# Prompt attention by position classes modulo 4, with scores in two halves of the TensorE array

## The reference

```
h = RMSNorm(x);  [u, Bg, Cg, q/k/v per head group, g_a, g_b] = h @ w_in
A = W_conv_out( Bg * dwconv3_causal( Cg * u ) )
B = W_attn_out( merge_g softmax-attn_g(q_g, k_g, v_g) )
x = x + W_o( sigmoid(g_a) * A + sigmoid(g_b) * B )
[up, gate] = RMSNorm(x) @ w_ffn_in;  x = x + W_down( silu(dwconv3_causal(gate) + b) * up )
```

## Time and profile before

| | |
|---|---|
| median of three runs | 1507.2 us |
| lowest and highest | 1506.79 and 1508.65 us |
| the profiled execution, its own time | 1507.49 us |
| its span, from the first to the last instruction | 1505.9 us |
| PE busy | 1492.0 us, 99% |
| DVE busy | 921.7 us, 61% |
| ACT busy | 743.9 us, 49% |
| mean granted clock of PE | 0.997 |

### The profile page before, as it was taken

The page is one execution under the profiler, slowest core; times in us unless marked ns, Lnnn a source line. Parts: engine busy times, 40 slices in busy tenths (PEclk is TensorE's granted clock), DMA queues, the critical chain, the costliest instruction groups (busy, mean ns, idle before and its releaser), DMA issues.

```text
span 1505.9 us, 31542 instructions
## 1 busy us (share of the span) xinstructions
PE 1492.0 (99%) x12434; PEld 1489.5 (99%) x12434; DVE 921.7 (61%) x1154; ACT 743.9 (49%) x751; POOL 76.4 (5%) x144
## 2 busy tenths in 40 slices
PE   8999999999999999999999999999999999999997
PEld 8999999999999999999999999999999999999997
DVE  8748487756667446667666565664444666556564
ACT  7555554544555344455555454454444554445452
POOL 2000001001221000100000000000000000000000
PEclk9999999999999999999999999999999999999998
DMA  7767667557888766554687876775556666665552
GB/s 277 267 187 242 200 186 241 155 161 210 236 250 249 255 182 182 179 184 160 194 261 240 252 230 215 252 250 184 182 182 182 182 182 182 180 184 193 182 183 100
DMA packets 145305, 308.58 MB, mean 205 GB/s; under 512 B 10128, under 2 KB 10384, under 8 KB 144672
## 3 DMA queue, kind: packets, MB, share of 16 engines
q1 hardware_dynamic: 139264, 268.73, 57.4%
q0 software_dynamic: 5920, 38.05, 7.6%
HBM read 301.32 MB, written 26.38 MB: 218 GB/s over the span
## 4 chain that ended last, share of the span: by engine, by line
PE 97%; DVE 2%; DMA 1%; SPq 0%; ACT 0%; issue 0%; DVEq 0%
PE acc L1009 71%; PE acc L1019 8%; PE acc L1021 8%; PE acc L1020 8%; DVE w_split L594 1%; DMA raw<-w_in 1%; PE side L1080 0%; PE side L1101 0%; DVE part L621 0%; DVE yg L987 0%; PE side L1148 0%; PE side L1091 0%; DVE h_rows L612 0%; PE side L1202 0%; ACT w_split L380 0%
## 5 line engine op out<-in xcount | busy, mean ns | idle before, releaser
L380 ACT ACTIVATE w_split<-raw 128x1024 fp32r<-128x1024 f32 x503 | 591.7, 1183 | 660.0 <-PE acc L1009 535.3
L594 DVE TENSOR_TENSOR w_split<-raw,w_split 128x1024 fp32r<-128x1024 f32 x503 | 616.4, 1234 | 478.1 <-ACT w_split L380 472.1
L1009 PE MATMUL acc<-h_rows,w_split 128*128 128x264 f32 x6480 | 791.5, 284 | 1.6 <-DVE w_split L594 1.6
L1009 PEld LDWEIGHTS acc<-h_rows,w_split 128*128 128x128 f32 x6480 | 784.0, 194 | 2.2 <-issue 1.8
L1009 PE MATMUL acc<-f_rows,w_split 128*128 128x264 f32 x1728 | 209.1, 284 | 0.0
L1009 PEld LDWEIGHTS acc<-f_rows,w_split 128*128 128x128 f32 x1728 | 208.4, 194 | 0.0
L1019 PE MATMUL acc<-h_rows,w_split 128*128 128x264 f32 x712 | 202.6, 285 | 1.0 <-DVE w_split L594 0.6
L1021 PE MATMUL acc<-h_rows,w_split 128*128 128x264 f32 x712 | 203.3, 286 | 0.0
L1020 PE MATMUL acc<-h_rows,w_split 128*128 128x264 f32 x712 | 202.5, 284 | 0.0
L1019 PEld LDWEIGHTS acc<-h_rows,w_split 128*128 128x128 f32 x712 | 137.5, 193 | 1.7 <-issue 1.6
L1021 PEld LDWEIGHTS acc<-h_rows,w_split 128*128 128x128 f32 x712 | 138.1, 194 | 0.0
(11 more groups left out here) (205 smaller groups left out, 1008.2 us busy)
## 6 DMA issues: line engine op xcount, KB each, us to landing
raw<-w_in SPq DMA_DIRECT2D x183, 512.0 KB, 3.7
raw<-w_ffn_in SPq DMA_DIRECT2D x176, 512.0 KB, 4.4
raw<-w_ffn_down SPq DMA_DIRECT2D x88, 512.0 KB, 3.7
raw<-w_out SPq DMA_DIRECT2D x32, 512.0 KB, 4.2
s_kv<-cache POOLq DMA_DIRECT2D x16, 1020.0 KB, 8.9
raw<-w_conv_out SPq DMA_DIRECT2D x16, 512.0 KB, 5.3
raw<-w_attn_out SPq DMA_DIRECT2D x8, 512.0 KB, 3.8
s_kv<-cache POOLq DMA_DIRECT2D x8, 508.0 KB, 4.8
```

The costliest lines, as they stand in the source:

```text
L380: act.activation(w_hi[:, s % RING], raw[:, s % RING], ACT.Copy).then_inc(hi_ready, 1)
L594: dve.tensor_tensor(w_lo[:, s % RING], raw[:, s % RING], w_hi[:, s % RING].bitcast(F32), ALU.subtract).then_inc(lo_ready, 1)
L1009: mm = pe.matmul(backwards(acc[:, m, 0:T]), w[:, slot, k, m * P:(m + 1) * P], row, start=False, stop=False)
```

## The change

The units stay heads times parity, but the 128 queries of a parity are ordered by their class modulo 4: first the 64 positions with remainder `odd`, then the 64 with remainder `odd + 2`. Groups 2 and 3 then need only the 64 keys of the query's own class.

- Scores become six matmuls: for each group two with 64 stationary columns (the queries of one class), whose outputs go to partitions 0 to 63 and 64 to 127. They have 256 moving columns for group 1 and 64 for groups 2 and 3, so a unit has 384 columns of scores instead of 512. Operands of one class are read at every fourth position.
- The unit's DVE and ACT operations have 384 columns, and three blocks are transposed instead of four. The third block holds the keys of group 2 in rows 0 to 63 and those of group 3 in rows 64 to 127.
- The values of groups 2 and 3 of one class share a block of `vtok`. The output is two matmuls with 128 moving columns, and two with 64 (one for each class), all with 128 stationary columns.
- `turn_values` has the same number and size of transposes, with every fourth position read for groups 2 and 3. DVE writes `att_hi` and `att_lo` at every fourth position, in two runs of 64.
- The mask table shrinks from 1024 to 768 columns.

```diff
+CLASSES = 4
+CLASS = SEQ // CLASSES
+UNIT_KEYS = SEQ + (NG - 1) * CLASS
...
-        vtok = place("vtok", [P, 2, NG * HEADS * HEAD_DIM])
+        vtok = place("vtok", [P, 2 + CLASSES, HEADS * HEAD_DIM])
...
+                    else:
+                        cls, d, to = n // 8, n // 2 % 4, n % 2
+                        keys = slice(cls + CLASSES * STRIP * to, cls + CLASSES * STRIP * (to + 1), CLASSES)
+                        row = CLASS * (g - 1) + STRIP * to
+                        out = vtok[row:row + STRIP, 2 + cls, :]
...
-                        cols = slice(odd, SEQ, 2)
+                        def by_class(rows):
+                            return rows[:, h, 0:SEQ].rearrange("p (i c) -> p c i", c=CLASSES)[:, odd:CLASSES:2, :]
+
+                        by_query = att_f[:, :].rearrange("p (c i) -> p c i", i=CLASS)
...
                 for g in range(NG):
-                    keys, first, n = (slice(0, SEQ), 0, SEQ) if g == 0 else (odd, P * (g + 1), P)
-                    mm = pe.matmul(side[:, SCORES + first:SCORES + first + n],
-                                   qkv[:, 12 * g + h, odd], qkv[:, 12 * g + 4 + h, keys], start=True, stop=True)
+                    for c in range(2):
+                        own = slice(odd + 2 * c, SEQ, CLASSES)
+                        keys, col, n = (slice(0, SEQ), 0, SEQ) if g == 0 else (own, SEQ + CLASS * (g - 1), CLASS)
+                        mm = pe.matmul(side[CLASS * c:CLASS * (c + 1), SCORES + col:SCORES + col + n],
+                                       qkv[:, 12 * g + h, own], qkv[:, 12 * g + 4 + h, keys], start=True, stop=True)
                 mm.then_inc(scores_done, 1)
...
-                blocks = ((0, 0), (0, 1)) + tuple((g, odd) for g in range(1, NG))
-                for b, (g, kb) in enumerate(blocks):
-                    mm = pe.matmul(side[:, HEAD_OUT:HEAD_OUT + P],
-                                   vtok[:, kb, (g * HEADS + h) * HEAD_DIM:(g * HEADS + h + 1) * HEAD_DIM],
-                                   prob_t[:, P * b:P * (b + 1)], start=b == 0, stop=b == len(blocks) - 1)
+                own = slice(h * HEAD_DIM, (h + 1) * HEAD_DIM)
+                for b in range(2):
+                    pe.matmul(side[:, HEAD_OUT:HEAD_OUT + P], vtok[:, b, own], prob_t[:, P * b:P * (b + 1)],
+                              start=b == 0, stop=False)
+                for c in range(2):
+                    mm = pe.matmul(side[:, HEAD_OUT + CLASS * c:HEAD_OUT + CLASS * (c + 1)], vtok[:, 2 + odd + 2 * c, own],
+                                   prob_t[:, SEQ + CLASS * c:SEQ + CLASS * (c + 1)], start=False, stop=c == 1)
                 mm.then_inc(head_done, 1)
```

More of the change, by code:

```diff
@@ L38 @@
 NG = len(GROUPS)
-assert all(d % 2 == 0 for _, d in GROUPS[1:])
+assert all(d % 4 == 0 for _, d in GROUPS[1:])
 SUB_WIN = 128
@@ L111 @@
 PAR_N = PAR_FB + FT
-UNIT_KEYS = 2 * P + (NG - 1) * P
+CLASSES = 4
+CLASS = SEQ // CLASSES
+UNIT_KEYS = SEQ + (NG - 1) * CLASS
 MASK_N = 2 * UNIT_KEYS
@@ L694, in turn_values @@
                 for n in range(first, last):
[L695 to L699, removed]
+                    if g == 0:
+                        half, d, to = n // 16, n // 4 % 4, n % 4
+                        keys = slice(half * P + STRIP * to, half * P + STRIP * (to + 1))
+                        out = vtok[STRIP * to:STRIP * (to + 1), half, :]
+                    else:
[3 more added lines that the diff above has]
+                        out = vtok[row:row + STRIP, 2 + cls, :]
                     dve.transpose(out.rearrange("p (h d) -> p h d", h=HEADS)[:, :, STRIP * d:STRIP * (d + 1)],
@@ L754, in _ @@
                         dve.wait_ge(att_f_ready, u + 1)
-                        dve.tensor_copy(att_hi[:, h, cols], att_f[:, :]).then_inc(att_hi_ready, 1)
+                        dve.tensor_copy(by_class(att_hi), by_query).then_inc(att_hi_ready, 1)
                         dve.wait_ge(att_hi_ready, u + 1)
-                        dve.tensor_tensor(att_lo[:, h, cols], att_f[:, :], att_hi[:, h, cols].bitcast(F32),
+                        dve.tensor_tensor(by_class(att_lo), by_query, by_class(att_hi).bitcast(F32),
                                           ALU.subtract).then_inc(att_ready, 1)
@@ L1071, in scores @@
             def scores(u):
-                h, odd = u // 2, slice(u % 2, SEQ, 2)
+                h, odd = u // 2, u % 2
                 if u == 0:
@@ L1362, in mask_table @@
     for odd in range(2):
-        q = np.arange(odd, SEQ, 2)[:, None]
+        q = np.concatenate([np.arange(odd + 2 * c, SEQ, CLASSES) for c in range(2)])[:, None]
         for g, (_, d) in enumerate(GROUPS):
-            k = np.arange(SEQ)[None, :] if g == 0 else np.arange(odd, SEQ, 2)[None, :]
+            k = np.arange(SEQ)[None, :] if g == 0 else q % CLASSES + CLASSES * np.arange(CLASS)[None, :]
             dist = q - k
```

## The result

The changed kernel takes 1513.42 us (median of five runs, 1512.73 to 1514.17) against 1507.91 (1506.79 to 1508.65) before: ratio 1.0034, 95% interval 1.0023 to 1.0045. It is slower by 5.5 us; when both were run again beside the experiments it was 4.7 us. The forecast was 1507.3, no change, and the range ended at 1509.4.

A forecast was written before the change was run, and what follows sets the result against it. PE was taken to set the time almost everywhere. Scores +0.96, stride +0.1, transposes -0.86, output 0, DVE and ACT -0.1 summed to +0.1 us: 1507.3 us on the median, no measurable change, range 1505.2 to 1509.4.

The forecast's parts named there:

- Cost 0: DVE's value transposes at line 700: if stride four slows each by 0.11 us, DVE's idle time takes it in, 0 us.
- Groups 2 and 3 ... I take 0.058: Scores on PE: four records of 64 columns in each half at 0.058 us each, 0.23 us together.
- The term of +0.96 us: All scores on PE: 1.03 us a unit against 0.91 before, so 0.12 more in a unit, 0.96 in eight.
- a rival with a chance of 0.17: Scores' short records take twice the time, by loads taking turns or stride four: +1.7 or +1.8 us, 1509.0 us; chance 0.17.
- the switch into and out of the narrow tiles: Around each unit's scores on PE: changing the tiling drains the array; two switches cost about 0.35 us.
- the halves side by side: Scores on PE: weight loads of both 64-column halves run at once; in turn would add 0.22 us a unit, 1.8 in eight.
- the transposes: PE's transposes in each attention unit: one of four goes, saving 0.108 us a unit, 0.86 us in eight.
- the output: PE's output matmuls in each unit: eight loads of 128 stationary columns stay 0.112 us apart, so nothing is saved.
- the clock: PE's granted clock should stay full, as line 1148's narrow stretch of 3.7 us was granted 1.00.
- The pause at 244.4: PE's wait while DVE takes the u group from PSUM: shrinks or goes with shorter exponentials, -0.1 us, once.
- the halves that don't overlap: Scores on PE: two 64-column tiles over all 128 rows run in turn, +5.3 us in eight, 1512.6 us; chance 0.06.

## Why the prediction was wrong

Two steps failed, and both are about reading every fourth position.

1. **"Cost 0" for DVE** is the larger error. The size of the slower transpose was right: 0.11 us worked out from lines 621 and 809, 0.104 measured. What failed is the cover. I took the last idle time ahead of the u group as a fixed point and counted seven transposes behind it. In the trace of the kernel before it is 0.26 us long:

```profile
233.90 1.63 DVE L700 STREAM_TRANSPOSE vtok<-qkv 32x128 f32<-32x128 f32 x5
235.79 1.23 DVE L594 TENSOR_TENSOR w_split<-raw,w_split 128x1024 fp32r<-128x1024 f32 x1 [0.26 <-ACT w_split L380]
237.05 1.64 DVE L700 STREAM_TRANSPOSE vtok<-qkv 32x128 f32<-32x128 f32 x5
```

Between it and the idle time before it, at 220.3, stand the 25 transposes of slots 0 to 4. Each takes 0.105 us more, 2.6 us in all, so DVE comes to this point late and the idle time is gone. An estimate from these rows: 32 transposes gain 3.4 us; less the idle times of 0.26 and 0.59 and the 0.3 saved at lines 739 and 743 leaves 2.2 us, and the two pauses behind it measured 1.46 and 0.69. And I looked at one place alone. The other was the end of the k phase, where 32 slower transposes run into 3.7 us of rotary work and then the tiles that PE waits for. Its pauses were 0.74 and 0.40 us. The term put at nothing cost 3.1 us in the profile (four pauses less the 0.2 of before), and 3 to 4 us by the pairs of experiments.
2. **"Groups 2 and 3 ... I take 0.058"** in the scores was mis-sized. The term of +0.96 us came out as +3.3. I had the stride inside a rival with a chance of 0.17, and priced it at the four short records alone, 1.7 us; it cost 8 x 0.30 = 2.4. It also lengthens the step behind the load that nothing hides, the first narrow one after the switch (from 0.27 to 0.33 us), and the way out of the last stream. Short pairs went at 0.10 to 0.12, and eight times 0.41 us is 3.3.

The Trainium skill, page Advanced Engine Details and Errata, Memory Cachelines, has the rule that I gave too little weight: 16-byte lines, two hits wanted on each. These runs agree in direction: strides of one and two were alike on DVE, and a stride of four cost in all three places. Pairs paced by their loads took about 0.118 instead of 0.058 us, a pair of 64-column passes 0.097 instead of 0.056, a DVE transpose 407 instead of 303 ns. None of them tests the length of a line as such.

What held: the switch into and out of the narrow tiles (scores with contiguous operands 1.02 us against 1.03 worked out); the halves side by side; the transposes, -0.11 in a unit; the output, whose loads of 128 stationary columns set 0.11 us for 64 moving columns as for 128; and the clock, granted in full through the attention of the changed kernel. The pause at 244.4, which I expected to shrink, was right only without the slower transposes.

Of the rivals, the halves that don't overlap gave 1512.6 us, near the 1513.4 measured, but by the wrong mechanism: the records of a pair start 0.007 us apart. The sum that did happen, a stride rival at 2.4 instead of 1.7 us and a DVE that loses its cover, was in none of them.

The experiments point to no version that beats the kernel before. With every strided read gone the change is worth nothing, and its one saving is 0.9 us. An estimate from these pieces: two units' scores under one pair of switches, from operands laid out by class, would save 4 x 0.35 = 1.4 us on the 0.1 that the change costs without the stride, so 1.3 us on the kernel before, less what the layout costs. It was not tried.

## What to carry to other kernels

Ask of each edit what stride its operands get on every engine, not only how many columns they have: halving the columns while doubling the stride gave nothing back here. Where an engine gets slower, don't look for cover at one point; add its whole new lateness from the last point at which it would still be idle, and do so at every place where the bounding engine takes something from it. Where it must do more, put the work into the phase in which it waits for others. And read the granted clock behind a new pause: behind DVE's late tiles it had fallen in two runs here, which cost 1.5 us on top of the pauses.

## What the runs showed of the hardware

- Reading fp32 at every fourth position: a 64-column weight load took 204 ns instead of 137 (median), a pair of 64-column passes 0.097 us instead of 0.056, a DVE transpose of 32 by 128 took 404 to 407 ns instead of 303, while every second position cost DVE nothing and PE 5 ns. DVE's operations that write every fourth position in two runs of 64 took 290 ns where those that write every second took 232, for 128 elements; with one operand also read so, 406 instead of 293.
- Two 64-column tiles over all 128 rows load and stream at the same time in full; leaving one of them out saved 0.01 us of 1.32.
- Each of the two records of a fp32 matmul with 128 stationary columns takes 0.11 us for 128, 64 or one moving column.
- The granted clock fell from 1.00 to 0.50 for 3.4 us after PE had stood for 2.6 and then 0.7 us (transposes spread over more slots), and after 1.7 and 0.7 us (no halves). It didn't after 1.5 and 0.7 us in the changed kernel, nor after 1.8 and 0.7 us in the kernel before with the slower transposes. At 0.50 a matmul of 264 moving columns started every 0.22 us, at 1.00 every 0.12.
